# Expert blocks with fixed groups: one 128-slot block per expert group fetched by plain transfers, three more with gathered weights

## The reference, cut to what matters

```python
g_val, g_idx = lax.top_k(g_prob, 1)
e_val, e_idx = lax.top_k(jax.nn.softmax(e_sel, axis=-1), TOP_K_IN_GROUP)
for gi in range(N_GROUPS):
    a = jnp.einsum('td,edf->tef', t, e_gate[gi])
    u = jnp.einsum('td,edf->tef', t, e_up[gi])
    hid = jax.nn.silu(a) * u * combine[:, gi, :, None]
    out = out + jnp.einsum('tef,efd->td', hid, e_down[gi])
```

## Time and profile before

| | |
|---|---|
| Median of 3 runs | 2111.68 us (2108.8 to 2114.98) |
| Profiled execution | 2114.34 us |
| Its span, first to last instruction | 2112.5 us |
| Mean granted PE clock | 0.925 of full |
| PE / DVE / ACT / POOL busy | 1849.6 / 1330.5 / 779.2 / 496.4 us |

### The profile page before, as it was taken

One profiled execution on the slowest core, in us unless ns is written; L12 is line 12 of the kernel. 1 busy time (PEld: TensorE's weight loads), 2 busy tenths in 40 slices (PEclk: granted clock), 3 DMA queues, 4 the chain that ended last, 5 costly groups with the idle time before them and its releaser, 6 DMA issues. The chain is left out here.

```text
span 2112.5 us, 21287 instructions
## 1 busy us (share of the span) xinstructions
PE 1849.6 (88%) x8780; PEld 1447.2 (69%) x8780; DVE 1330.5 (63%) x1664; ACT 779.2 (37%) x994; POOL 496.4 (23%) x417
## 2 busy tenths in 40 slices
PE   4999878789699999699999996998688897789985
PEld 3778756677697888477888784776554574677774
DVE  3235588879545343566235455798978565798995
ACT  3343334332003123343123223324246433666663
POOL 1030066767242000110000001433200000544440
PEclk8999887789899999899999997999889998899997
DMA  6121020002001223134334341221110111989893
GB/s 224 62 80 61 20 80 0 1 21 85 16 2 60 80 100 126 54 140 163 148 147 180 140 159 41 85 100 60 60 60 1 40 40 48 358 341 349 338 352 148
DMA packets 37329, 241.35 MB, mean 114 GB/s; under 512 B 4192, under 2 KB 4704, under 8 KB 10736
## 3 DMA queue, kind: packets, MB, share of 16 engines
q1 hardware_dynamic: 23984, 147.69, 18.9%
q0 software_dynamic: 13248, 92.30, 11.4%
HBM read 228.39 MB, written 11.58 MB: 114 GB/s over the span
## 5 line engine op out<-in xcount | busy, mean ns | idle before, releaser
L336 PE MATMUL bank<-h_high,wsplit 128*128 128x512 f32 x992 | 323.4, 405 | 25.6 <-POOL wsplit L1339 8.6
L1339 DVE TENSOR_TENSOR wsplit<-ring,wsplit 128x2048 fp32r<-128x2048 f32 x77 | 177.4, 2304 | 182.0 <-ACT wsplit L821 181.9
L821 ACT ACTIVATE wsplit<-ring 128x2048 fp32r<-128x2048 f32 x98 | 186.9, 1907 | 212.3 <-PE bank L336 188.3
L336 PEld LDWEIGHTS bank<-h_high,wsplit 128*128 128x128 f32 x992 | 190.3, 192 | 79.9 <-POOL wsplit L1339 9.5
L336 PE MATMUL bank<-xn_high,wsplit 128*128 128x512 f32 (+1 forms) x832 | 219.9, 352 | 27.0 <-DVE wal_low L1390 18.5
L336 PE MATMUL bank<-h_low,wsplit 128*128 128x512 f32 x496 | 199.5, 402 | 0.0
L336 PEld LDWEIGHTS bank<-xn_high,wsplit 128*128 128x128 f32 x832 | 148.3, 194 | 49.3 <-issue 19.9
L336 PE MATMUL bank<-f_high,wsplit 128*128 128x512 f32 x512 | 166.3, 405 | 4.4 <-DVE f_low L1759 4.4
L2227 POOL TENSOR_TENSOR x<-x,z 128x512 f32<-128x512 f32 x8 | 12.8, 1594 | 598.8 <-DVE z L1697 598.8
L336 PE MATMUL bank<-xn_low,wsplit 128*128 128x512 f32 (+1 forms) x416 | 145.6, 350 | 0.0
L1799 DVE SCALAR_TENSOR_TENSOR conv<-conv_in,vecs,conv 128x512 f32<-128x512 f32 x120 | 140.5, 1171 | 4.3
(11 more groups left out here) (465 smaller groups left out, 3890.2 us busy)
## 6 DMA issues: line engine op xcount, KB each, us to landing
ring<-in_W SPq DMA_DIRECT2D x122, 1024.0 KB, 4.8
xslot<-zeros SPq DMA_DIRECT2D x7, 516.0 KB, 5.0
block<-xslot SPq DMA_DIRECT2D x7, 516.0 KB, 11.0
yslot<-block_out SPq DMA_DIRECT2D x7, 512.0 KB
x_in<-in_xT SPq DMA_DIRECT2D x4, 528.0 KB, 7.4
x<-in_xT SPq DMA_DIRECT2D x2, 1024.0 KB, 6.2
out_y<-h_tokens SPq DMA_DIRECT2D x4, 512.0 KB, 2.6
bc<-in_bc SPq DMA_DIRECT2D x1, 1024.0 KB, 4.7
```

Of the source, the lines that this page charges most:

```text
L336: return g.matmul(o, l, r, start=first, stop=last_, skip_group_check=True)
L821: g.activation(wst[:, side(n), 0, :], ringt[:, n % RING, :], ACT.Copy).then_inc(*a.sig(("high", n)))
L1339: g.tensor_tensor(wst[:, side(n), 1, :], ringt[:, n % RING, :], hi, SUB).then_inc(*t.sig(("low", n), ("released", n)))
```

## The change

Block g, for g from 0 to 3, is now always group g's own, and holds its first 128 tokens. Tokens past the 128th of a group go to one of three further blocks, 4 to 6 (`past` marks them). Since the first four blocks have known groups, their 48 pieces are fetched by plain transfers from POOL's queue, which need no indices. Pieces 36 and up of blocks 4 to 6 are still fetched by index. The first six pieces are issued ahead of the routing: pieces 0 to 2 as soon as the ring's slots are free, pieces 3 to 5 after the event `("end", "mix2", "dve")`, the last DVE work before the routing. The scatters now stand behind six fetches on POOL and not two, and `gather(6)` no longer waits for block 0. On ACT and DVE `parts_for(0)` stands ahead of `turn_block(0)`. Four more constant columns, 128 x g, move the later SBUF tiles by 8 words.

```diff
-MC = 128 + 2 * 12 + NB
+MC = 128 + 2 * 12 + NB + 4
...
+            parts_for(0)
             turn_block(0)
...
-            g.tensor_scalar(nb, ng, 0.0, None, ALU.is_gt).then_inc(*v.sig())
-            for lim in (128.0, 256.0, 384.0):
+            g.tensor_scalar(nb, ng, 128.0, None, ALU.is_gt).then_inc(*v.sig())
+            for lim in (256.0, 384.0):
                 v.wait_ge(*v.own())
                 g.scalar_tensor_tensor(out=nb, in0=ng, scalar=lim, in1=nb, op0=ALU.is_gt, op1=ADD).then_inc(*v.sig())
-            g.memset(s4[:, 0:1], 0.0).then_inc(*v.sig())
+            g.memset(s4[:, 0:1], 4.0).then_inc(*v.sig())
...
-            g.tensor_scalar(RO["s128"], s4, 128.0, None, MUL).then_inc(*v.sig())
-            v.wait_ge(*v.own())
-            g.tensor_tensor(rk[:, 0:4, :], rk[:, 0:4, :], RO["s128"].unsqueeze(1).to_broadcast([128, 4, 4]), ADD).then_inc(*v.sig())
+
+            g.tensor_scalar(RO["s128"], s4, 128.0, -128.0, MUL, ADD).then_inc(*v.sig())
+            v.wait_ge(*v.own())
+            past, own_ = RO["past"], MCT[:, 152 + NB:156 + NB]
+            g.tensor_tensor(RO["s128"], RO["s128"], own_, SUB).then_inc(*v.sig())
+            g.tensor_scalar(past, rk[:, 0:4, :], 128.0, None, ALU.is_ge).then_inc(*v.sig())
+            v.wait_ge(*v.own())
+            g.tensor_tensor(past, past, RO["s128"].unsqueeze(1).to_broadcast([128, 4, 4]), MUL).then_inc(*v.sig())
+            g.tensor_tensor(rk[:, 0:4, :], rk[:, 0:4, :], own_.unsqueeze(1).to_broadcast([128, 4, 4]), ADD).then_inc(*v.sig())
+            v.wait_ge(*v.own())
+            g.tensor_tensor(rk[:, 0:4, :], rk[:, 0:4, :], past, ADD).then_inc(*v.sig())
...
             def gather(c):
                 n, kind, i = STREAM[c]
-                x = 4 + 12 * n + COLS.index((kind, i))
+                x = COLS.index((kind, i))
                 if c >= NS:
                     q.wait_ge(*at("part", c - NS))
                 elif c < RING:
                     q.wait_ge(*at("low", max(n for n in SPL if n % RING == c)))
-                g.indirect_dma_start(slots[c % NS], None, wmoe, indexed(x)).then_inc(slot_landed[c % NS], 16)
-
-            q.wait_ge(*at("weight_rows"))
-            gather(0)
-            gather(1)
+                else:
+                    q.wait_ge(*at("end", "mix2", "dve"))
+                if n < 4:
+                    r = 128 * (8 * n + i if kind == "ex" else 32 + 4 * n + i)
+                    g.dma_start(slots[c % NS], wmoe[r:r + 128, :]).then_inc(slot_landed[c % NS], 16)
+                else:
+                    q.wait_ge(*at("weight_rows"))
+                    g.indirect_dma_start(slots[c % NS], None, wmoe, indexed(4 + 12 * n + x)).then_inc(slot_landed[c % NS], 16)
+
+            for c in range(NS):
+                gather(c)
             q.wait_ge(*at("ht_out", 3))
             q.wait_ge(*at("token_rows"))
             q.wait_ge(*at("token_weights"))
             q.wait_ge(slots_cleared, 16 * NB)
             for m in range(4):
                 g.indirect_dma_start(xslot, indexed(m), HT[:, m, :], None).then_inc(rows_scattered, 16)
-            q.wait_ge(*at("end", "routing", "pe"))
-            q.wait_ge(*at("end", "routing", "act"))
-            q.wait_ge(*at("end", "routing", "dve"))
-            q.wait_ge(block_landed[0], 16)
-            for c in range(2, NG):
+            for c in range(NS, NG):
                 gather(c)
             q.wait_ge(y_stored, 16 * NB)
             q.wait_ge(rows_scattered, 64)
```

More of the change, by code:

```diff
@@ L271, in program @@
         HB, RW, MCT = tile("hb", 0, 8, 512), tile("router", 10240, 8, 36), tile("moe_cst", 10528, MC)
-        LT, L, HT = tile("logits_t", 10688, 512), tile("logits", 11200, 4, 36), tile("h_tokens", 11344, 4, ROW)
-        RT, IX = tile("routing", 15472, 640), tile("indices", 16112, NB * 12 + 4).bitcast(I32)
-        XTK, ROWS, dg = tile("x_tokens", 16200, 4, 1024), tile("rows", 20296, 2, 1024), tile("diag", 22344, 2, 128)
+        LT, L, HT = tile("logits_t", 10696, 512), tile("logits", 11208, 4, 36), tile("h_tokens", 11352, 4, ROW)
+        RT, IX = tile("routing", 15480, 640), tile("indices", 16120, NB * 12 + 4).bitcast(I32)
+        XTK, ROWS, dg = tile("x_tokens", 16208, 4, 1024), tile("rows", 20304, 2, 1024), tile("diag", 22352, 2, 128)
         XS = tile("block", 0, 2, ROW)
@@ L277, in program @@
         XL = [tile(f"block_low{z}", 4112 + 1024 * z, 8, 128, dt=F32R) for z in range(2)]
-        w3 = [tile(f"parts{z}", 22344 + 4096 * z, 2, 2048, dt=F32R) for z in range(2)]
+        w3 = [tile(f"parts{z}", 22352 + 4096 * z, 2, 2048, dt=F32R) for z in range(2)]
         YS, PD = tile("block_out", 6160, 2, 512), tile("hidden", 7184, 2, 512)
@@ L281, in program @@
         NS, NP, NG = RING + 3, 4, NB * 12
-        slots = [ringt[:, k, :] for k in range(RING)] + [tile(f"slot{k}", 30536 + 2048 * k, 2048) for k in range(NS - RING)]
+        slots = [ringt[:, k, :] for k in range(RING)] + [tile(f"slot{k}", 30544 + 2048 * k, 2048) for k in range(NS - RING)]
         parts = [wst[:, 0], wst[:, 1]] + w3
@@ L308, in program @@
         for _name, _dims in (("gm", (4,)), ("km", (4,)), ("sg", (4,)), ("gv", (4,)), ("m1", (4,)), ("m2", (4,)), ("sw", (4,)),
-                             ("og", (4, 4)), ("eg", (4, 4)), ("es", (4, 8)), ("es2", (4, 8)), ("exx", (4, 8)), ("o1", (4, 8)),
+                             ("og", (4, 4)), ("eg", (4, 4)), ("past", (4, 4)), ("es", (4, 8)), ("es2", (4, 8)), ("exx", (4, 8)), ("o1", (4, 8)),
                              ("o2", (4, 8)), ("wn", (4, 8)), ("tmp4", (4, 8, 4)), ("rk", (8, 4)), ("nb", (4,)), ("s4", (4,)),
@@ L2388, in constants @@
         m[:, 140 + n] = 1024 if kind == "ex" else 512
-    m[:, 152:] = np.arange(NB)
+    m[:, 152:152 + NB] = np.arange(NB)
+    m[:, 152 + NB:] = 128 * np.arange(4)
     return np.concatenate([c[n] for n, _ in CST], axis=1).astype(np.float32), m.astype(np.float32)
```

## The result

The changed kernel took 2119.54 us (median of 6 runs, 2119.09 to 2122.41), the kernel before 2114.18 us beside it (6 runs, 2108.8 to 2116.97). The ratio is 1.0029, with an interval of 1.0016 to 1.0043: about 5.4 us slower, and above the forecast range. The forecast counted from a kernel before at 2111.68 us, and the one beside the changed kernel took 2.5 us more; measured from its own kernel before, the loss of 5.4 us is near the range's upper edge (5.8 us above 2111.68) and far from the forecast difference of -0.2.

A forecast was written before the change was run, and what follows sets the result against it. PE was taken as the bound, with a 3.06 us gap at each block boundary. +1.45 at the first product and -1.57 given back made -0.1 us; from the median of 2111.68 the forecast was 2111.5 us, range 2105 to 2117.5.

The forecast's parts named there:

- What bounds the blocks: In the blocks: PE is the bound, with a gap of 3.06 us at each boundary, not the transfers.
- The rival that saw transfers as the bound: In the blocks: transfers bind, four fewer pieces have to come, 11.9 us less, 2099.8 us; chance 0.07.
- The routing, +0.4 us: In the routing: one DVE instruction fewer, four more for the slots; all that follows comes 0.4 us later.
- The early fetches, 0: Before the routing: six early pieces delay neither router weights nor scatters; 0 taken, 3 us as the bound.
- The first product, +1.45 from the order: Start of the blocks: `block_low` stands behind four DVE splits, so PE's first expert product comes 1.45 us later.
- Given back, -1.57: Start of the blocks: with no wait for a piece, 1.57 us is recovered by the third group of products.
- POOL's plain transfers, 0: In the blocks: plain transfers stay hidden if each takes under 3.2 us, cost 0; rival of slower ones, chance 0.07.
- The rest: From 1829.77 on: same instructions, order and waits, no wait for transfers, boundary gap stays 3.06 us, tail unchanged.
- the rival of the low clock: At block boundaries: 1.5 us more per slow one; four turned fast 2105.5, two more slow 2114.6; chance 0.10 in all.

The follow-up runs named there:

- E1: Kernel before, with a block's output bank handed out again last, so PE does not wait for `block_out`: 2092.13 us, ratio 0.9908.
- E2: Changed kernel, with a block's output bank handed out again last: 2088.09 us, ratio 0.9895.
- E9: Changed kernel with the old order of splits, pieces 0 and 1 fetched plain after `weight_rows`, the others after block 0 landed: 2109.77 us, ratio 0.9992.
- E4: Changed kernel without the order edit, so the first block's own split comes first, then piece 0: 2109.26 us, ratio 0.9995.
- E12: Kernel before, with the output bank handed out last and later SBUF tiles moved by 8 words: 2086.57 us, ratio 0.9881.
- E16: Changed kernel with 13 unused products put on PE in the first boundary gap alone: 2112.10 us, ratio 1.0004.
- E10: The changed kernel itself run again, with no edit: 2116.58 us, ratio 1.0024.
- E7: Changed kernel with 13 unused products put on PE in each boundary gap: 2106.76 us, ratio 0.9969.
- the filled kernel before: Kernel before with 13 unused products put on PE in each boundary gap: 2105.94 us, ratio 0.9969.
- E5: Kernel before with only its later SBUF tiles moved by 8 words (32 bytes): 2111.36 us, ratio 0.9996.
- E14: Changed kernel with a DVE product in the routing done eight further times, making that chain 3.2 us longer: 2110.32 us, ratio 1.0014.
- E3: Changed kernel with two pieces split ahead of the first block's own split, not four: 2114.42 us, ratio 1.0013.
- E11: Changed kernel with the output bank handed out last and only two pieces split ahead of the first block's own: 2086.86 us, ratio 0.9874.

## Why the prediction was wrong, by its own steps

- **What bounds the blocks: right.** PE with a gap of 3.06 us, not the transfers: 18.4 us in six waits in both kernels, and 373 to 381 GB/s reached once the gaps were gone (E1, E2). The rival that saw transfers as the bound is refuted. The Trainium skill's rule that the HBM side binds at about 358 GB/s ("DMA: Bandwidth & Descriptors", section "Where 436 GB/s comes from") does not agree with these rows: they moved more than that for 215 us.
- **The routing, +0.4 us: right.** From the copy of the logits to the token weights it is 13.62 us against 13.26.
- **The early fetches, 0: right.** The router's products start at 1768.98, not late; E9 against E4 puts their use at 0.2 us at the first product, and at nothing later.
- **The first product, +1.45 from the order: right as a mechanism.** PE waits for `block_low` behind four splits. The changed kernel against E4, which differs in nothing else, has 1.9 us (45.55 to 43.63). The sum's 1.45, which had the routing's 0.4 in it, was too small: the four splits start when `rows` ends, so the late `rows` (below) are passed on in full. The other 0.96 of the 2.88 are in E4 too, where the late `rows` hold up block 0.
- **Given back, -1.57: right in size.** 1.45 of 2.88 came back. The reason given, that ACT no longer waits for piece 3, holds, but E9 shows that plain fetches do it without being early.
- **POOL's plain transfers, 0: right.** 0.53 us each.
- **What was missed ahead of the blocks: 1.5 us.** I let the `rows` stage only follow the routing's 0.4 us. Its products ran mostly at 1.2 GHz, so the start is +1.43 at the first hidden value and not -0.1. I also wrote that SP loads block 0 once the scatters have landed; it waits for the end of `rows` too, and here that came last, so block 0 is transposed at T0 + 37.15 against + 35.92, 1.2 us later and not 0.4. Leaving the delayed ones out, the last `rows` ends late (T0 + 32.8 or more, against 31.7) in two of five kernels with the old routing, E1 and E12, and in eight of nine with the new one, all but E16; that the routing's few tenths tip it is likely, but only argued.
- **The step that failed: "The rest", and the rival of the low clock beside it.** I wrote that the boundary gap stays 3.06 us, which it does, and took the cost of a boundary to be 38.65 or 40.21 as in the earlier trace rows, so 1.5 us at most for each that turns slow, with 0.10 for all of it. There is a third level, 41.0 us, with 12 products in 5.49 us, 2.7 us above the full clock's 38.3. Three of five reached it, and in E10 all five. Against before that is 3.44 us in the periods and 0.71 in the last leg, or 12.2 us of low clock behind the gaps against 6.2, less what the moved tiles give. The filled gaps (E7) take it away: 38.3 five times, and the changed kernel is level with the filled kernel before. The mechanism was in the list of rivals, at too low a price (3 us for two more slow boundaries) and too low a chance, and there "mostly faster".
- **What the sum left out: the moved tiles.** They take 0.27 us off a period at full clock (E5), about 1.5 us over the blocks, where the sum has nothing. They hid part of the loss.
- **What stays open.** Which pattern of clocks a kernel falls into. It differs between two executions of one kernel (the changed one and E10), so one profile of a kernel can't tell what an edit does to it. Taking the order edit out did take the loss out in these runs (E4, level with before). But E14, with the edit and a delay, is nearly level too (1.0014, 0.9998 to 1.0030), and E3, with another order, has all five at 41 us. So that the order edit brings the low clock is not shown. What it costs besides is 1.9 us at the first product, of which 1.3 are left at block 1 (the changed kernel against E4), and about as much at the gather back where no clock is in play (E2 against E12, which has the routing's 0.4 us in it).

## What to carry to other kernels

A short idle time of TensorE that comes back at each turn of a loop can cost more than its length, and the amount differs between turns and between two executions of one kernel: here 0, 1.5 or 2.7 us on top of 3.06. Look at the granted clock behind each such gap, and remove the gap before tuning anything by half a per cent; handing out the output's PSUM bank last made it vanish, and is worth 19 and 23 us (E1 and E2 against 2111.11, the median of before beside them), while the change under study, in that version and at the same placement, makes the blocks 1.3 us slower (E2 against E12). Judge an edit at the start of a phase in a version without such gaps, where what it gains at the start is kept (E11 against E2: 3.7 us by G). The fastest versions, E11 and E12, need 2086.86 and 2086.57 us, some 1.2% less than before, and cannot be told apart by these runs.

## What the hardware showed that was not expected

- 12 products of 128x512 behind a gap of 3.06 us took 3.02, 4.27 or 5.49 us in one execution, with a granted clock of 1.00 for the shortest and 0.50 for the longest.
- Moving a tile by 32 bytes made products that read it 390 ns instead of 396, and those that read `wsplit`, which did not move, stayed at 396 (E5).
- A plain 1 MB fetch keeps POOL for 0.53 us, an indexed one up to 3.05.
